# Gate and up of a split-fp32 feed-forward: seven block products for eight

## The reference, cut to what matters

```
z  = rms_norm(x, norm_mix) @ w_in          # u, q, k, v
h  = x + concat(pool_mixer(u), banded_attention(q, k, v)) @ w_out
hn = rms_norm(h, norm_ffn)
y  = h + (silu(hn @ w_gate) * (hn @ w_up)) @ w_down     # 1024 -> 2816 -> 1024
```

## Time and profile before

| | |
|---|---|
| median of three runs | 2284.66 us |
| profiled execution, its own time | 2285.82 us |
| its span, first to last instruction | 2284.0 us |
| TensorE busy | 2227.1 us (98%) |
| VectorE busy | 868.4 us (38%) |
| ScalarE busy | 701.7 us (31%) |
| GpSimd busy | 609.5 us (27%) |
| mean granted TensorE clock | 0.99 |
| DMA | 195.50 MB, mean 86 GB/s |

### The profile page before, as it was taken

The page is one execution under the profiler, slowest core; times in us unless marked ns, Lnnn a source line. Parts: engine busy times, 40 slices in busy tenths (PEclk is TensorE's granted clock), DMA queues, the critical chain, the costliest instruction groups (busy, mean ns, idle before and its releaser), DMA issues.

```text
span 2284.0 us, 32102 instructions
## 1 busy us (share of the span) xinstructions
PE 2227.1 (98%) x13246; PEld 2030.9 (89%) x13246; DVE 868.4 (38%) x1500; ACT 701.7 (31%) x1756; POOL 609.5 (27%) x282
## 2 busy tenths in 40 slices
PE   6999999988999899999999999999999999999999
PEld 6888888866878899999999999999999999999997
DVE  5565565561111233332332333233333233233334
ACT  5666666542333221121212121122212121212111
POOL 1000000061442224232433233232423232232321
PEclk9999999989999999999999999999999999999999
DMA  6011111035654431222222531222122422222121
GB/s 174 27 40 47 38 38 33 20 116 161 213 173 132 129 125 56 74 74 65 66 74 65 166 125 58 72 74 71 59 74 74 161 71 73 64 66 74 56 74 69
DMA packets 233498, 195.50 MB, mean 86 GB/s; under 512 B 20605, under 2 KB 209834, under 8 KB 233354
## 3 DMA queue, kind: packets, MB, share of 16 engines
q1 hardware_dynamic: 230954, 184.80, 25.8%
q10 hardware_dynamic: 2400, 8.65, 1.0%
HBM read 158.50 MB, written 35.03 MB: 85 GB/s over the span
## 4 chain that ended last, share of the span: by engine, by line
PE 91%; DMA 2%; ACT 2%; SPq 2%; DVE 2%; POOL 1%; issue 1%; ACTq 0%
PE ps L639 27%; PE ps L641 27%; PE ps L640 27%; PE ps L735 2%; PE ps L709 2%; PE ps L823 1%; PE ps L721 1%; SPq L368 1%; PE ps L653 1%; DMA xt_lo_raw<-mix_d 1%; PE ps L825 1%; PE ps L821 1%; PE ps L697 1%; DMA w_lo_raw<-in_w_gate 1%; ACT s_sb L972 1%
## 5 line engine op out<-in xcount | busy, mean ns | idle before, releaser
L573 POOL TENSOR_TENSOR w_lo<-w_lo_raw,w_hi 128x1024 fp32r<-128x1024 f32 x198 | 470.7, 2405 | 1042.3 <-ACT w_hi L1038 521.8
L639 PE MATMUL ps<-xb_hi,w_hi 128*128 128x352 f32 x2112 | 686.6, 325 | 7.0 <-POOL w_lo L573 4.1
L641 PE MATMUL ps<-xb_lo,w_hi 128*128 128x352 f32 x2112 | 684.7, 324 | 0.0
L640 PE MATMUL ps<-xb_hi,w_lo 128*128 128x352 f32 x2112 | 683.8, 324 | 0.0
L639 PEld LDWEIGHTS ps<-xb_hi,w_hi 128*128 128x128 f32 x2112 | 398.0, 188 | 8.8 <-issue 7.4
L640 PEld LDWEIGHTS ps<-xb_hi,w_lo 128*128 128x128 f32 x2112 | 400.0, 189 | 1.2
L641 PEld LDWEIGHTS ps<-xb_lo,w_hi 128*128 128x128 f32 x2112 | 397.5, 188 | 0.0
L1059 ACT ACTIVATE sg<-ps 128x352 f32<-128x352 f32 x132 | 61.2, 464 | 1061.0 <-PE ps L641 1060.9
L1275 DVE TENSOR_TENSOR aa<-ps,sg 128x352 f32<-128x352 f32 x132 | 69.2, 525 | 817.6 <-PE ps L641 789.5
L1294 DVE TENSOR_TENSOR h<-ps,h 128x512 f32<-128x512 f32 (+1 forms) x396 | 273.0, 689 | 189.8 <-PE ps L641 187.5
L641 PE MATMUL ps<-w_lo,act_hi 128*128 128x512 f32 x660 | 257.1, 390 | 0.0
(11 more groups left out here) (102 smaller groups left out, 2295.2 us busy)
## 6 DMA issues: line engine op xcount, KB each, us to landing
w_lo_raw<-in_w_gate SPq DMA_DIRECT2D x66, 512.0 KB, 3.7
w_lo_raw<-in_w_up SPq DMA_DIRECT2D x66, 512.0 KB, 3.8
w_lo_raw<-in_w_down SPq DMA_DIRECT2D x66, 512.0 KB, 4.3
xb_lo_raw<-hn_d SPq DMA_DIRECT2D x3, 2816.0 KB, 10.6
xload<-in_x_prompt SPq DMA_DIRECT2D x16, 512.0 KB, 4.4
mix_d<-o_st SPq DMA_DIRECT2D x64, 128.0 KB, 1.8
xt_lo_raw<-mix_d SPq DMA_DIRECT2D x16, 512.0 KB, 6.2
wg_hi_raw<-in_x_prompt SPq DMA_DIRECT2D x16, 512.0 KB, 6.7
```

Source lines behind the costliest of these rows:

```text
L573: nc.gpsimd.tensor_tensor(lo, raw, hi.bitcast(F32), ALU.subtract).then_inc(done, 1)
L639: nc.tensor.matmul(out, s_hi, m_hi, start=first, stop=False)
L640: nc.tensor.matmul(out, s_lo, m_hi, start=False, stop=False)
L641: return nc.tensor.matmul(out, s_hi, m_lo, start=False, stop=final)
```

## The change

A gate or up block of a group is one matrix product: 256 features by 1024 by 704 tokens. It is cut in two along each of the three directions, and the four result blocks (128 features by 352 tokens) come from seven block products instead of eight (Strassen's scheme in Winograd's form). A "set" s is one such product: 2G is gate, 2G+1 is up of group G, 66 sets. A block product m has 4 slices times 3 matmuls of 352 columns (`product`).

- *Weights.* Four of the seven left operands are sums or differences of weight blocks, made on VectorE (`weight_sum`, 128x512, both inputs in SBUF); the other three are blocks as loaded. ScalarE makes seven high parts per set (`high2(s, m)`), GpSimd seven low parts (`low2(s, m)`). A set's high part m goes into the place of the last set's m, so it waits for that product.
- *Rows.* The same for the right operands, once per part of 704 tokens: `rows_sum` four times, `rows_high` seven times, `rows_low` four times on VectorE and three times on GpSimd, 128x1408 each. They have one buffer: their sums and high parts for the next part wait for the last set's products, and their low parts are made while `down` runs.
- *Results.* The products 0, 1, 2 start a bank each (`BANK_OF`); 3 adds to the bank of 0, 5 to that of 1, 4 and then 6 to that of 2. Before product 3, ScalarE copies product 0 (`save_p1`); before 4, VectorE has made `u2` from product 2; before 5, `q7` from product 1; before 6, the first `result_sum`. Product 2 of the next set waits for the second `result_sum` (c21_read), product 1 for the reader of result 0. Three of four products gate times up now have both inputs in SBUF.
- *Order.* `load_gate_up(2G + 2)` stands behind `load_down(G)` in SP's queue. TensorE: products(2G), down(G-1), products(2G+1), but down(G-1) first where a part begins. `act_hi` and `act_lo` have one buffer instead of two. `down` starts its first two token tiles after three low parts. The stores of y move from ScalarE's queue to SP's.

The diff's core, eight leading blanks left out of each line:

```
+SETS = 2 * NG
+PRODUCTS = 7
+BANK_OF = (0, 1, 2, 0, 2, 1, 2)
+A_BLOCK = {0: (0, 0), 3: (0, 1), 5: (1, 1)}
+RESULTS = ((0, 0), (1, 1), (1, 0), (0, 1))
+X_HIGHS = (0, 1, 4, 2, 3, 5, 6)
+X_LOWS_DVE = (0, 2, 4, 6)
+X_LOWS_POOL = (1, 3, 5)
...
+    def load_gate_up(s):
+        if s == 0:
+            sp.wait_ge(xn_ready, NTILES)
+        elif s == 1:
+            sp.wait_ge(out_ready, 2 * NTILES)
+        else:
+            sp.wait_ge(product_done, after_product(s - 2, 5))
+        a = 256 * (s // 2 % GROUPS)
+        for i in range(2):
+            load(w2_raw[s % 2][:, i].rearrange("p j (k m) -> p (j k) m", k=HALF_K),
+                 (w_gate_k, w_up_k)[s % 2][:, :, a + PART * i:a + PART * (i + 1)], w2_loaded[s % 2])
...
+        if G > 0:
+            load_gate_up(2 * G + 1)
+            if j == 0:
+                store_y(p - 1)
+            load_down(G)
+            if j == 0:
+                for i in range(PT_TILES):
+                    load_h(p, i)
         if j == 1 and p + 1 < PARTS:
-            load_xb(p + 1)
-        if j == 0 and p > 0:
-            for i in range(PT_TILES):
-                load_h(p, i)
-        if 1 <= G < NG - 1:
-            load_down(G)
+            load_second_halves(p + 1)
+        if j == GROUPS - 1 and p + 1 < PARTS:
+            load_first_halves(p + 1)
+        if G + 1 < NG:
+            load_gate_up(2 * G + 2)
...
+    for m in range(PRODUCTS):
+        low2(0, m)
+    for s in range(SETS):
+        G, which = divmod(s, 2)
         p, j = divmod(G, GROUPS)
-        if G >= 1:
-            low1(G - 1)
-        low2(G + 1, range(4 if G + 1 < NG else 2))
-        if 2 <= j < 2 + KT and p + 1 < PARTS:
-            xb_low(p + 1, j - 2)
+        for m in range(PRODUCTS):
+            if s + 1 < SETS:
+                low2(s + 1, m)
+            if m == 2 and which == 1:
+                low1(G)
+        if which == 1 and j == GROUPS - 1 and p + 1 < PARTS:
+            for m in X_LOWS_POOL:
+                rows_low(p + 1, m)
...
+    def product(s, m):
+        p = s // (2 * GROUPS)
+        pe.wait_ge(w2_split, PRODUCTS * s + m + 1)
+        if s % (2 * GROUPS) == 0:
+            if m in X_LOWS_DVE:
+                pe.wait_ge(xs_split_dve, 4 * p + X_LOWS_DVE.index(m) + 1)
+            else:
+                pe.wait_ge(xs_split_pool, 3 * p + X_LOWS_POOL.index(m) + 1)
+        if m == 0:
+            need(pe, c12_read, s - 1)
+        elif m == 1:
+            need(pe, c11_read, s)
+        elif m == 2:
+            need(pe, c21_read, s)
+        else:
+            pe.wait_ge((p1_saved, u2_ready, q7_ready, c22_read)[m - 3], s + 1)
+        lo = low_of(s, m)
+        for k in range(HALF_K):
             cols = slice(PART * k, PART * (k + 1))
-            hi, lo = xb_hi[p % 2][:, k, tok], xb_lo[p % 2][:, k, tok]
-            last = split_products(out, w2_hi[:, slot, cols], w2_lo[:, slot, cols], hi, lo, k == 0, k == KT - 1)
-        last.then_inc((g_ready, u_ready)[which], 1)
-    def gate_up(G):
-        for n in range(4):
-            for which in range(2):
-                gate_up_unit(G, n // 2, n % 2, which)
+            last = split_products(product_bank(s, m), w2_hi[:, m, cols], lo[:, cols], xs_hi[:, m, k], xs_lo[:, m, k],
+                                  m < 3 and k == 0, k == HALF_K - 1, partial=True)
+        last.then_inc(product_done, 1)
...
+        if G % GROUPS == 0:
+            down(G - 1)
+        products(2 * G)
+        if G % GROUPS > 0:
+            down(G - 1)
+        products(2 * G + 1)
...
-    def high2(G, slots):
-        for n in slots:
-            act.wait_ge(w2_loaded[n], 16 * (G + 1))
-            nc.scalar.activation(w2_hi[:, n], w2_raw[:, n], ACT.Copy).then_inc(w2_high, 1)
+    def high2(s, m):
+        if s == 0:
+            act.wait_ge(wo_free, 1)
+        else:
+            act.wait_ge(product_done, after_product(s - 1, m))
+        if m in A_BLOCK:
+            act.wait_ge(w2_loaded[s % 2], 32 * (s // 2 + 1))
+        else:
+            act.wait_ge(w_sum, 4 * s + {1: 1, 2: 2, 6: 3, 4: 4}[m])
+        nc.scalar.activation(w2_hi[:, m], raw_of(s, m), ACT.Copy).then_inc(w2_high, 1)
...
+    def save_p1(s):
+        act.wait_ge(product_done, after_product(s, 0))
+        need(act, c12_read, s - 1)
+        nc.scalar.activation(p1[:, s % 2, :], product_bank(s, 0), ACT.Copy).then_inc(p1_saved, 1)
+    def gate(G, n):
+        s = 2 * G
+        if n == 0:
+            act.wait_ge(product_done, after_product(s, 3))
+            need(act, c11_read, s)
+            nc.scalar.activation(sg[:, 0, :], product_bank(s, 3), ACT.Silu).then_inc(c11_read, 1)
+        else:
+            act.wait_ge((c22_read, c21_read, c12_read)[n - 1], s + 1)
+            nc.scalar.activation(sg[:, n, :], sg[:, n, :], ACT.Silu).then_inc(silu_done, 1)
     def high_part(G, n):
-        act.wait_ge(a_done, 4 * G + n + 1)
-        c, nb = divmod(n, 2)
-        nc.scalar.activation(act_hi[:, G % 2, c, NB * nb:NB * (nb + 1)], aa[:, n % 2, :], ACT.Copy).then_inc(ah_done, 1)
...
+    for s in range(SETS):
+        G, which = divmod(s, 2)
         p, j = divmod(G, GROUPS)
-        gates(G)
-        high2(G + 1, (2, 3) if G == 0 else range(4 if G + 1 < NG else 2))
-        if 2 <= j < 2 + KT and p + 1 < PARTS:
-            xb_highs(p + 1, j - 2)
-        if j == 0 and p > 0:
-            store_y(p - 1)
...
+        save_p1(s)
+        for m in range(3):
+            if s + 1 < SETS:
+                high2(s + 1, m)
+        if which == 1:
+            high1(G)
...
+        for n in range(4):
+            if s == 0 and n < 2:
+                stage_copy(NTILES - 1, n)
+            if which == 0:
+                gate(G, n)
+            else:
+                high_part(G, n)
+            if s + 1 < SETS:
+                high2(s + 1, n + 3)
+        if which == 1 and j == GROUPS - 1 and p + 1 < PARTS:
+            for m in X_HIGHS:
+                rows_high(p + 1, m)
...
+    def weight_sum(s, n):
+        m = (1, 2, 6, 4)[n]
+        if n == 0:
+            dve.wait_ge(w2_loaded[s % 2], 32 * (s // 2 + 1))
+        else:
+            dve.wait_ge(w_sum, 4 * s + n)
+        if s == 0:
+            dve.wait_ge(wo_free, 1 if n == 0 else 2)
+        elif n != 2:
+            dve.wait_ge(product_done, after_product(s - 1, m))
+        raw = w2_raw[s % 2]
+        a, b, op = ((raw[:, 0, 0], raw[:, 1, 0], ALU.subtract),
+                    (raw[:, 1, 1], raw_of(s, 1), ALU.subtract),
+                    (raw[:, 0, 1], raw_of(s, 2), ALU.subtract),
+                    (raw[:, 1, 0], raw[:, 1, 1], ALU.add))[n]
+        nc.vector.tensor_tensor(raw_of(s, m), a, b, op).then_inc(w_sum, 1)
...
+    def q7_sum(s):
+        dve.wait_ge(product_done, after_product(s, 1))
+        dve.wait_ge(p1_saved, s + 1)
+        nc.vector.tensor_tensor(q7[:, :], product_bank(s, 1), p1[:, s % 2, :], ALU.add).then_inc(q7_ready, 1)
+    def u2_sum(s):
+        dve.wait_ge(product_done, after_product(s, 2))
+        nc.vector.tensor_tensor(u2[:, :], product_bank(s, 2), p1[:, s % 2, :], ALU.add).then_inc(u2_ready, 1)
+    def result_sum(s, n):
+        m = (4, 5, 6)[n - 1]
+        dve.wait_ge(product_done, after_product(s, m))
+        dve.wait_ge((q7_ready, u2_ready, p1_saved)[n - 1], s + 1)
+        if s % 2 == 0:
+            out = sg[:, n, :]
+            need(dve, a_done, 3 * s // 2)
+        else:
+            out = aa[:, n % 2, :]
+            need(dve, al_done, 2 * (s - 1) + n - 1)
+        nc.vector.tensor_tensor(out, product_bank(s, m), (q7[:, :], u2[:, :], p1[:, s % 2, :])[n - 1], ALU.add)\
+            .then_inc((c22_read, c21_read, c12_read)[n - 1], 1)
+    def act_product(G, n):
+        s = 2 * G + 1
+        if n == 0:
+            dve.wait_ge(c11_read, s)
+            dve.wait_ge(product_done, after_product(s, 3))
+            need(dve, al_done, 4 * G - 1)
+            nc.vector.tensor_tensor(aa[:, 0, :], product_bank(s, 3), sg[:, 0, :], ALU.mult).then_inc(c11_read, 1)
+            return
+        dve.wait_ge((c22_read, c21_read, c12_read)[n - 1], s + 1)
+        dve.wait_ge(silu_done, 3 * G + n)
+        nc.vector.tensor_tensor(aa[:, n % 2, :], aa[:, n % 2, :], sg[:, n, :], ALU.mult).then_inc(a_done, 1)
...
+    def gate_sums(s):
+        q7_sum(s)
+        weight_sum(s + 1, 0)
+        u2_sum(s)
+        weight_sum(s + 1, 1)
+        weight_sum(s + 1, 2)
+        result_sum(s, 1)
+        weight_sum(s + 1, 3)
+        result_sum(s, 2)
+        result_sum(s, 3)
+    def activations(s):
+        G, p, more = s // 2, s // (2 * GROUPS) + 1, s + 1 < SETS
+        new_part = more and (s + 1) % (2 * GROUPS) == 0
+        q7_sum(s)
+        if more:
+            weight_sum(s + 1, 0)
+        u2_sum(s)
+        if more:
+            weight_sum(s + 1, 1)
+            weight_sum(s + 1, 2)
+        act_product(G, 0)
+        if new_part:
+            rows_sum(p, 0)
+        result_sum(s, 1)
...
+        low_part(G, 0)
+        act_product(G, 1)
+        if more:
+            weight_sum(s + 1, 3)
+        if new_part:
```

(84 more changed lines are left out.)

276 lines of the change are left out of this document (149 added, 127 removed).

## The result

The changed kernel takes 2502.94 us (median of four runs, 2495.08 to 2512.49), the kernel before 2284.93 on the same chip: 1.095 times as long, 95% interval 1.090 to 1.100. The forecast was 2415 us, slower; the direction held, the time lies 88 us above it and 23 us above the range.

The account below looks back on a forecast made before the run. TensorE was taken to bound the kernel, 98% busy. Span 2284.0 - 128.3 (matmuls) - 10 (start) + 30 x 6.5 (waits) + 30 x 0.5 (clock) + 58 (part changes) + 2.5 = 2416; stated 2415 us, range 2250 to 2480.

Parts of the forecast that it names:

- The matmuls: Gate and up sets on TensorE: 24 of 192 matmuls fewer per group, 0.162 us each, saving 128.3 us.
- the period that the forecast built on: One group of 256 features on TensorE, before waits and clock losses are added: 42.6 us.
- The port: Up and next gate set: two-input VectorE operations wait out GpSimd's SBUF-reading instructions; TensorE waits 0.6, 3.35 and 1.0 us.
- the clock: TensorE at 1.2 GHz behind product 3's wait in the gate set: 0.5 us per pair (0 to 1.7).
- changes of part: Two switches of 704 tokens: late weight load, row sums and low parts delay TensorE, 29 us each, 58 for two.
- The rival in which the port does not bind: VectorE slips between GpSimd's low parts, only the late load waits, 1.57 us per pair: about 2240 us, chance 0.19.
- the milder chain: Waits of 5.0 or 3.8 us per pair, no clock loss, part changes 20 each: 2300 to 2340 us, chance 0.22.
- product 3's wait: Gate set: TensorE waits for ScalarE's late `save_p1` before product 3, 3.35 us per pair.
- GpSimd loses next to nothing: Earlier trace, four w_down low parts in a row: 9.67 us for 4 x 2.41, so GpSimd is not fully blocked.
- The 45 us: Extra if VectorE also blocks GpSimd fully: its chain some 3 us longer per pair, half on the path; left out.
- The load that comes late: Up set: gate weights queued behind w_down land at 8.1 us, so product 4 starts 1.57 us late (0.4 to 2).
- product 4's second wait: Gate set: `u2` comes late behind VectorE's list, so product 4 starts at 27.9 for 26.9, 1.0 us.

Follow-up runs that it names:

- 4: Changed kernel with the next gate columns loaded ahead of w_down and GpSimd filling the weights' low parts with zeros instead of subtracting: 2176.59 us, 0.9517 of the kernel before.
- Experiment 5: Changed kernel, gate load first, each weight low part replaced by three zero fills as long as the subtraction, without SBUF reads: 2175.2 us, 0.9515 of the kernel before.
- experiment 3: Changed kernel with GpSimd filling the low parts of gate, up and down weights with zeros instead of subtracting: 2309.64 us, 1.0109 of the kernel before.
- 1: Changed kernel with SP issuing the next gate columns ahead of the w_down pair instead of behind it: 2353.25 us, 1.0289 of the kernel before.
- Experiment 11: Changed kernel with the gate load first, plus 14 unneeded matmuls ahead of product 3 of the gate sets only: 2324.56 us, 1.0167 of the kernel before.
- experiment 10: Changed kernel plus 14 unneeded matmuls ahead of product 3 in gate sets and product 4 in up sets: 2465.16 us, 1.0778 of the kernel before.

## Why the forecast held in its direction and missed in its size

**The matmuls.** 792 fewer, right. 0.160 us apart (0.162 forecast). Experiments 4 and 5 give the period that the forecast built on, 42.33 us for its 42.6, which is 10 us in all in the kernel's favour.

**The port.** Right in kind and size. By rows alone it was priced at 4.95 us per pair, 148 us, and 15 for the clock behind it, and it has a part in the 58 of the changes of part. Taking it away saves 193 us (3 against the changed kernel) or 177 (4 against 1). Experiment 5 shows that it is the reads. The rival in which the port does not bind is out, and with it the milder chain: product 3's wait is 3.11 us in the mean of the 30 pairs (3.35 forecast), 2.88 without the late load.

What failed in it is the reading that GpSimd loses next to nothing. The group of w_down's low parts in the changed kernel (count, then total us and mean ns), which took 2405 ns each in the earlier trace rows:

```profile
L678 POOL TENSOR_TENSOR w_lo<-w_lo_raw,w_hi 128x1024 fp32r<-128x1024 f32 x66 | 175.9, 2686 | 16.9 <-ACT w_hi L1167 16.9
```

From 745 us on, 219 low parts of 128x512 start while a VectorE operation with both inputs in SBUF is under way, and take 1.65 us in the mean; the 234 others take 1.29. VectorE's operation has 0.50 us left then, of which the two records share some 0.14. Even in the earlier trace rows the third of the four takes 2.66 us by the trace, which their sum of 9.67 hides. So the trace agrees with the Trainium skill ("SBUF — State Buffer", Who interferes with whom) in both directions: the engine that comes second is blocked, GpSimd for the rest of VectorE's short operation, VectorE for the rest of GpSimd's long one. By these means GpSimd's chain grew by 2.9 us per group, the 3 us that the forecast worked out and set aside. The 45 us that it put on this did not show: the port's whole price came out within 7 us of the forecast.

**The load that comes late.** This is the step that failed: right in kind, far too small. Forecast 1.57 us per pair (0.4 to 2), 47 us, and a share of the changes of part (7.3 us each, 15): 62. Taking it away saves 150 us (1 against the changed kernel) or 133 (4 against 3); within the 30 pairs that is 4.06 and 3.76 us each. Product 4's wait itself is 3.06 us in the mean, twice the forecast; nearly all of the rest is the half clock that it brings, for which this term had nothing. The forecast's port-free rival makes the same point: 2240 us with the load as only wait; experiment 3 is that kernel, and takes 2309.64. Four things were missed.
- *The landing.* The bulk of the data was right, and its end: 7.6 us after the issue of the w_down pair, from which the times here count. But the forecast let VectorE start 0.2 us after it. Windows at the end of two such loads, w_down issued at 1013.70 and at 2251.51 (DMA share and GB/s last), and the weight sum that starts on the second:

```profile
1020.70:1021.20 0.50, 0.50 (x5) 0.36 (x3) 0.00 (x0) 0.00 (x0) 0.00 (x0) 1.00 0.88 220
1021.20:1021.70 0.50, 0.15 (x1) 0.00 (x0) 0.00 (x0) 0.00 (x0) 0.00 (x0) 1.00 0.15 40
1021.70:1022.20 0.50, 0.00 (x0) 0.00 (x0) 0.00 (x0) 0.00 (x0) 0.00 (x0) 1.00 0.03 7
...
2258.50:2259.00 0.50, 0.50 (x5) 0.37 (x3) 0.00 (x0) 0.00 (x0) 0.00 (x0) 1.00 0.83 210
2259.00:2259.50 0.50, 0.16 (x2) 0.00 (x0) 0.00 (x0) 0.00 (x0) 0.00 (x0) 1.00 0.15 39
2260.00:2260.50 0.50, 0.00 (x0) 0.00 (x0) 0.00 (x0) 0.00 (x0) 0.00 (x0) 1.00 0.07 20
```

```profile
2261.48 0.69 DVE L1424 TENSOR_TENSOR ws_lo_raw<-w_lo_raw 128x512 f32<-128x512 f32 x1 [5.59 <-DMA w_lo_raw<-in_w_gate]
```

  Packets trail behind at a low rate, to 1021.89 in the one and to 2260.99 in the other; the load counts as landed 0.5 us after the last of them (1022.38, 2261.45), and the weight sum starts at once. Bulk to start is 1.1 us in the one and 2.4 in the other. Over the 25 up sets away from the starts and ends of the parts, the weight sum starts 8.27 to 10.38 us after the issue, 9.14 in the mean, where the forecast had 7.9 (8.1 from the set's start). Product 4 waits 2.76 us in the mean, 1.89 to 4.0.
- *The rows' second halves.* In the second group of the first two parts `load_second_halves` stands in SP's queue between the w_down pair and the gate load. Product 4 waits 7.34 and 6.70 us there. The forecast has no term for it.
- *The chain behind it.* What is late by the load partly stays late through the port: in the period shown product 2 waits 1.20 us and not 0.6, and without the late load 0.46; product 3 3.52, without it 2.86.
- *The clock behind it.* The forecast allowed half clock behind product 3's wait alone. Product 4's wait brought it too: in experiment 3, where it is the only wait, 93 us went by at half clock, and it came behind this wait in 16 of the 30 pairs. Two pairs in a row there have the same wait, 2.93 and 2.92 us, one with half clock behind it and one without. The waits, and the windows of the two whole pairs (PEclk is the last value but two):

```profile
1439.32 0.40 PE L752 MATMUL ps<-xs_hi,w_hi 128*128 128x352 f32 x1 [2.93 <-DVE u L1461]
1486.50 0.40 PE L752 MATMUL ps<-xs_hi,w_hi 128*128 128x352 f32 x1 [2.92 <-DVE u L1461]
```

```profile
1428.54:1475.74 47.20, 44.27 (x238) 41.08 (x237) 23.73 (x42) 14.73 (x26) 9.26 (x16) 0.96 0.22 68
1475.74:1521.11 45.37, 42.45 (x238) 39.28 (x236) 23.74 (x42) 14.74 (x26) 9.26 (x16) 1.00 0.24 70
```

  The stretch at half clock costs 1.8 us. In the changed kernel it came behind this wait in 13 of 30 pairs, and product 2 then did not wait at all.

**The clock.** The forecast priced product 4's second wait (1.0 us) and the half clock (0.5) together at 1.5 us; the slow product 3 cost 1.57 and swallowed that wait, as the forecast said it might. Experiment 11 shows the two trade places. Taking 167 of the 226 us at half clock out of the changed kernel gave 38 us (experiment 10); by the spacing of the matmuls (0.29 for 0.16) it would be 75, by the forecast's term for all of it 15.

**The changes of part.** 61.58 and 61.53 us for the two periods around the first: 123.1, less two of 42.6 and one pair's 7, is 31, and the same sum gives 30 at the second; forecast 29 each.

**The sum again.** The missing 77 us (2493.3 for 2416) lie inside the pairs. Mean time of the 30 pairs:

| | low parts subtracted | weights' low parts filled |
|---|---|---|
| late gate load | 52.18 us (changed kernel) | 46.50 (3) |
| gate load first | 48.12 (1) | 42.74 (4) |

The load costs 3.8 to 4.1 us per pair for the forecast's 1.57, 66 to 75 us too little over 30 pairs. The port costs 5.4 to 5.7 for 5.45 (4.95 and 0.5 of clock), at most 7 us too little. The shorter base gives 10 back. The two terms do not add up exactly, since each makes the other worse: apart they save 150 and 193 us, together 326.

Counted by TensorE's waits the sum looks better than it was. They come to 6.9 us per pair for the forecast's 6.5, because two errors met: product 4 waits 3.06 in the up set for 1.57, and 0.07 in the gate set for 1.0. What the forecast lacks by this count is behind the waits, some 5.9 us at half clock in each pair, against one stretch priced at 0.5. That the direction held is not luck, for the port, the larger part of the loss, was read rightly; with the load at its true price the sum would have been 2480 to 2490 us.

## What to carry to other kernels

When work is added to an engine that shares SBUF reads with another, look for the longest instruction of the other in the stretch, and not only at its total: with the load reordered, moving two of 2.4 us and leaving fourteen of 1.3 turned a loss of 2.9% into a gain of 3.2%. Price a load by the time at which its reader starts in the trace, over many repetitions, not by bytes over rate; and when it heads a chain, price the chain with it. Time at a low clock is only in part time lost: ask which wait it stands in for.
